# Cross scores as three fp32r products, decay rows fetched by ScalarE into one buffer, value products a unit later

## The chip, the cores and the metric

One core of one Trainium2 chip runs the kernel. The metric is the device time of one execution in microseconds (us), lower is better. TensorE (PE in the profile) multiplies matrices into PSUM, VectorE (DVE) and ScalarE (ACT) work elementwise, GpSimd (POOL) does small statistics, and SyncE (SP) issues most DMAs.

## The reference

Four encoder layers over 256 tokens of width 1024, all in fp32. Each layer is a mixer (a Mamba-2 state space mixer, differential attention, spatial gating, the state space mixer again) beside a cross attention to a memory of 256 rows; both are concatenated, projected and added to x, and a squared-ReLU MLP follows. The two parts that the change touches:

```python
def memory_cross_attention(q, mem_n, w_kv, gq, gk):      # 4 heads of 256
    k, v = jnp.split(mem_n @ w_kv, 2, axis=-1)
    q = rmsnorm(q.reshape(b, l, X_HEADS, X_HEAD_DIM), gq)
    k = rmsnorm(k.reshape(b, m, X_HEADS, X_HEAD_DIM), gk)
    s = jnp.einsum('blhd,bmhd->bhlm', q, k) * (X_HEAD_DIM ** -0.5)
    p = jax.nn.softmax(s, axis=-1)
    return jnp.einsum('bhlm,bmhd->blhd', p, v)

# ssd_chunked: within a chunk, per group g and head r
y_diag = jnp.einsum('bcgls,bcgrls,bcsgrp->bclgrp', cb, segsum_exp(adt), xdt)
```

`segsum_exp` is the exponential of a difference of cumulated sums, for every pair of positions. The kernel builds it from a "decay row" (the cumulated sums of one head along the free axis, on all partitions) less a per-partition column.

## The kernel before, in words

All weights are a stream of 570 units of 128 x 1024 fp32 (512 KB). SyncE loads unit u into `raw` (6 slots). ScalarE rounds it to fp32r in `w_hi_t` (line 1434, ring of 4), VectorE takes the rest, raw less high, into `w_lo_t` (line 1678), and TensorE multiplies each unit as three fp32r products: activations high x weights high, high x weights low, low x weights high (lines 1236 to 1238 for form `nat`, 1247 to 1249 for form `feat` with 256 columns, 1258 and 1265 for `wide`). A `nat` unit is 12 matmuls of 512 columns.

A planner in Python (class `Plan`, from line 112) writes one list of steps. Every engine goes through this list in order and does its own part of each step. Small work (transposes, norms, attention heads, state space groups) are Python generators, "threads", that advance once per weight unit: `yield 2` waits two units. A step placed at unit w is preceded on ScalarE and VectorE by the casts of the units up to w + 2, so each engine prepares weights about three units ahead of TensorE. `is_late` delays a step while the planner's summed costs (`COST`) for an engine lie over a limit. PSUM has 8 banks: pairs (0,1) and (2,3) alternate for weight units (`stream_job`), banks 4 to 7 are `misc` for small work. A `Job` holds banks and knows when ScalarE and VectorE have read them (counted in `act_free`, `dve_free`); the next user of the bank waits for that (`banks_free`).

The parts that matter here:

- **Keys and queries.** `normed` (line 304) multiplies four units into a pair of banks. `row_norm` then runs squares (ScalarE, line 1516), the inverse root (GpSimd), the product (VectorE, lines 1747 and 1749, step `norm_mul`), and two steps `nt_turn`: TensorE transposes (1293) and ScalarE copies to `qT` (1503) or `kT` (1506), both plain fp32. VectorE has no part in `nt_turn`.
- **A cross head** (`head`, line 333): `x_score` is four fp32 matmuls of 128 x 256 (line 1383), two token tiles x two halves of the 256 features; then `x_exp` (ScalarE 1623), `x_norm` (VectorE 1907, 1910), `x_turn` (TensorE 1392, ScalarE 1628, VectorE 1915 makes `xpT_lo`), and one unit later `x_out`: twelve fp32r matmuls of 128 x 256 against the values `v`, `v_lo` (1404 to 1406).
- **The first units.** The list begins with values 0 (units 0 to 3), values 1 (4 to 7), keys 0 (8 to 11), keys 1 (12 to 15). Values 0 and keys 0 share banks (0,1). The values' evacuation is ScalarE line 1529 and VectorE line 1922; it needs the memory's inverse root from GpSimd.
- **State space groups** (`ssm`, 8 groups in each of two layers). After step `decay`, ScalarE stores the cumulated sums to HBM (`cs_rows`, 1555). Step `ssd_r` is SyncE's: it waits for that store, and from the third group on for the exponentials of the group two before (`e_new`), and issues two broadcast loads of 256 KB into `gap[n % 2]` (line 1045), between two weight loads in its own order. `gap` has two pairs of buffers; the second pair lies in tiles 22 and 23 of `act_hi` and `act_lo`. Step `ssd_gap` on VectorE subtracts the column (line 1791, 8 instructions), placed in the same unit as `ssd_a` of the group before it. `ssd_a` has on ScalarE the two exponentials into `E` (1567), on VectorE `cbm` (1796); `ssd_m` multiplies (1802, 1807), `ssd_b` is TensorE's 1334 and 1340.
- **Output projection** (`out_projection`, line 484): two accumulators a and b of two banks; units go tile 0 a, tile 0 b, tile 1 a, tile 1 b, and so on.

## Time and profile before

| | us |
|---|---|
| median of 3 runs (1770.59 to 1770.93) | 1770.88 |
| the profiled execution, its own time | 1770.17 |
| its span, first to last instruction | 1768.4 |
| TensorE busy (9556 matmul records) | 1760.0 |
| VectorE busy | 1182.3 |
| ScalarE busy | 1005.3 |
| GpSimd busy | 220.0 |

The page gives busy time by engine, the chain of waits that ended last, and groups of like instructions. Matmuls overlap in the array: the duration of one record is longer than its share of TensorE's time, so what a matmul costs is read from the distance between neighbours in the timeline. Where records of one line are merged, "x8" is their number and the second column their stretch.

### The profile page before, as it was taken

How to read it: one execution, taken by the hardware profiler on the slowest of the kernel's cores; microseconds unless marked ns; L12 is line 12 of the kernel's file. 1: busy time of each engine (PE TensorE's matmuls, PEld its weight loads, DVE VectorE, ACT ScalarE, POOL GpSimd, SP SyncE). 2: the span in 40 equal slices, each digit the busy share in tenths (PEclk: the TensorE clock that was granted, in tenths of full speed). 3: DMA queues.
4: the chain of work that ended last, by engine and by line, in shares of the span. 5: the costliest groups of instructions: out<-in, count | busy, mean ns of one | idle time of the engine just before them, and what ended most of it. 6: DMA issues, size and time to landing. Idle time of an engine off the chain costs nothing.

```text
span 1768.4 us, 26013 instructions
## 1 busy us (share of the span) xinstructions
PE 1760.0 (100%) x9556; PEld 1518.9 (86%) x9556; DVE 1182.3 (67%) x1628; ACT 1005.3 (57%) x1598; POOL 220.0 (12%) x548
## 2 busy tenths in 40 slices
PE   9999999999999999999999999999999999999999
PEld 8998988888888888888888888888899998888887
DVE  5788876666665666656566566655678887656665
ACT  6667775544455675544465545444566777545443
POOL 2412231000012220000012300000131223100000
PEclk9999999999999999999999999999999999999999
DMA  7555543555555443555565445555557554355554
GB/s 271 171 204 186 179 143 122 181 190 191 191 186 180 156 141 121 177 191 191 191 213 180 160 136 182 191 191 191 190 168 215 177 173 150 122 190 189 191 191 143
DMA packets 90041, 314.03 MB, mean 178 GB/s; under 512 B 10176, under 2 KB 11584, under 8 KB 89920
## 3 DMA queue, kind: packets, MB, share of 16 engines
q1 hardware_dynamic: 89328, 311.27, 53.0%
q8 instruction: 80, 1.31, 0.3%
q10 hardware_dynamic: 592, 1.12, 0.2%
q14 instruction: 41, 0.34, 0.1%
HBM read 311.23 MB, written 1.11 MB: 177 GB/s over the span
## 4 chain that ended last, share of the span: by engine, by line
PE 96%; DVE 3%; ACT 1%; issue 1%; ACTq 0%; DVEq 0%
PE ps L1236 19%; PE ps L1238 19%; PE ps L1237 19%; PE ps L1258 13%; PE ps L1265 7%; PE ps L1247 3%; PE ps L1248 3%; PE ps L1249 3%; PE ps L1283 1%; PE ps L1383 1%; PE ps L1334 1%; PE ps L1293 1%; DVE w_lo_t L1678 1%; DVE xsT L1761 1%; DVE bcT L1761 1%
## 5 line engine op out<-in xcount | busy, mean ns | idle before, releaser
L1678 DVE TENSOR_TENSOR w_lo_t<-raw,w_hi_t 128x1024 fp32r<-128x1024 f32 x569 | 691.7, 1225 | 367.6 <-ACT w_hi_t L1434 367.0
L1434 ACT ACTIVATE w_hi_t<-raw 128x1024 fp32r<-128x1024 f32 x569 | 596.9, 1059 | 393.5 <-PE ps L1238 148.5
L1236 PE MATMUL ps<-w_hi_t,act_hi 128*128 128x512 f32 x832 | 327.7, 394 | 0.6 <-issue 0.6
L1237 PE MATMUL ps<-w_lo_t,act_hi 128*128 128x512 f32 x832 | 324.3, 390 | 0.0
L1238 PE MATMUL ps<-w_hi_t,act_lo 128*128 128x512 f32 x832 | 324.1, 390 | 0.0
L1258 PE MATMUL ps<-hT,w_hi_t 128*128 128x512 f32 x1024 | 256.0, 392 | 0.0
L1258 PEld LDWEIGHTS ps<-hT,w_hi_t 128*128 128x128 f32 x1024 | 185.9, 189 | 34.4
L1238 PEld LDWEIGHTS ps<-w_hi_t,act_lo 128*128 128x128 f32 x832 | 156.2, 188 | 33.1
L1236 PEld LDWEIGHTS ps<-w_hi_t,act_hi 128*128 128x128 f32 x832 | 156.4, 188 | 31.6 <-issue 1.0
L1237 PEld LDWEIGHTS ps<-w_lo_t,act_hi 128*128 128x128 f32 x832 | 156.5, 188 | 30.2
L1236 PE MATMUL ps<-w_hi_t,hT 128*128 128x512 f32 x416 | 165.7, 398 | 0.0
L1238 PE MATMUL ps<-w_hi_t,hT 128*128 128x512 f32 x416 | 162.4, 390 | 0.0
L1237 PE MATMUL ps<-w_lo_t,hT 128*128 128x512 f32 x416 | 162.1, 390 | 0.0
L1247 PE MATMUL ps<-hT,w_hi_t 128*128 128x256 f32 x512 | 149.1, 291 | 0.5 <-DVE w_lo_t L1678 0.5
L1265 PEld LDWEIGHTS ps<-hT,w_lo_t 128*128 128x128 f32 x1024 | 139.7, 190 | 10.0
L1249 PE MATMUL ps<-hT,w_lo_t 128*128 128x256 f32 x512 | 144.9, 283 | 0.0
L1248 PE MATMUL ps<-hT,w_hi_t 128*128 128x256 f32 x512 | 144.8, 283 | 0.0
L1265 PE MATMUL ps<-hT,w_lo_t 128*128 128x256 f32 x1024 | 142.8, 282 | 0.0
L1236 PE MATMUL ps<-w_hi_t,memT_hi 128*128 128x512 f32 x252 | 101.5, 403 | 0.9 <-issue 0.8
L1247 PEld LDWEIGHTS ps<-hT,w_hi_t 128*128 128x128 f32 x512 | 98.1, 192 | 2.1 <-issue 1.6
L1248 PEld LDWEIGHTS ps<-hT,w_hi_t 128*128 128x128 f32 x512 | 98.2, 192 | 0.4
L1238 PE MATMUL ps<-w_hi_t,memT_lo 128*128 128x512 f32 x252 | 98.5, 391 | 0.0
(225 smaller groups left out, 2279.2 us busy)
## 6 DMA issues: line engine op xcount, KB each, us to landing
raw<-in_wstream SPq DMA_DIRECT2D x569, 512.0 KB, 3.3
gap<-cs_rows SPq DMA_DIRECT2D x32, 256.0 KB, 4.8
mix<-in_mem SPq DMA_DIRECT2D x4, 256.0 KB, 5.2
x<-in_x SPq DMA_DIRECT2D x1, 1024.0 KB, 9.1
raw<-in_wstream SPq DMA_DIRECT2D x2, 256.0 KB, 4.1
wsT<-in_sgu_wT ACTq DMA_DIRECT2D x1, 512.0 KB, 3.6
sgain<-in_sgu_gain ACTq DMA_DIRECT2D x1, 512.0 KB, 5.9
out<-x SPq DMA_DIRECT2D x1, 512.0 KB, 2.8
```

Source lines behind the costliest of these rows:

```text
L1236: pe.matmul(o, ah, wh[:, n], start=first and c == 0, stop=False)
L1237: pe.matmul(o, ah, wl[:, n], start=False, stop=False)
L1238: mm = pe.matmul(o, al, wh[:, n], start=False, stop=last and c == UK - 1)
L1247: pe.matmul(o, wh[:, n], ah, start=first and c == 0 and f % 2 == 0, stop=False, skip_group_check=True)
L1248: pe.matmul(o, wh[:, n], al, start=False, stop=False, skip_group_check=True)
L1249: mm = pe.matmul(o, wl[:, n], ah, start=False, stop=last and c == UK - 1, skip_group_check=True)
L1258: pe.matmul(o.rearrange("p (a b) -> p a b", a=2), wh[:, n], hT2[:, :, kt, :], start=first and c == 0, stop=False, skip_group_check=True)
L1265: mm = pe.matmul(o[:, 0:SEQ], wl[:, n], hT2[:, 0, kt, :], start=False, stop=last and c == UK - 1, skip_group_check=True)
L1283: mm = pe.transpose(ps[:, bf, f * SEQ + t * P:f * SEQ + (t + 1) * P], src[:, t, (2 * m + f) * P:(2 * m + f + 1) * P], ident)
L1434: act.activation(w_hi_t[:, u % RING, :], raw[:, u % SLOTS, :], ACT.Copy).then_inc(w_hi, 1)
L1678: dve.tensor_tensor(w_lo_t[:, u % SLOTS, :], raw[:, u % SLOTS, :], w_hi_t[:, u % RING, :].bitcast(F32), ALU.subtract)\
L1761: ins = dve.scalar_tensor_tensor(out=dst[:, f, d:SEQ], in0=ps[:, job.banks[h], (f % 2) * SEQ:(f % 2 + 1) * SEQ - d], scalar=col("conv_w", ...
```

## The change

Three things at once. (1) `qT` and `kT` become fp32r high parts; `nt_turn` gets a VectorE step that writes low parts `qT_lo`, `kT_lo` (into tiles 16 to 23 of `act_hi` and `act_lo`, where the heads' results go later); a score is three fp32r products per token tile and feature half, twelve matmuls, and waits for VectorE as well. (2) The decay rows are fetched by ScalarE into one pair of buffers: the first group's in step `ssd_r`, the later ones at the end of the group before's exponentials in `ssd_a`; VectorE's `ssd_gap` and GpSimd's `ssd_xd` move to three units after `ssd_a`. (3) `x_out` is placed two units after `x_turn` in place of one; the very first key block takes banks (6,7); the output projection begins with tile 0 a, tile 1 a, tile 0 b, tile 1 b. The squares of the spatial gating layer get an fp32 view of `qT`'s memory.

```diff
-... "x_score": (0, 0.7, 1.72)
+... "x_score": (0, 0.7, 1.44)
...
             for m in range(2):
-                tj = self.misc_job(True, False)
+                tj = self.misc_job(True, dst in ("qT", "kT"))
+                if tj.dve:
+                    self.work(0, 0.7, 0)
                 self.step("nt_turn", m=m, nt=job.dve, dst=dst, tile=tile + 2 * m, gain=gain, job=tj)
-            self.ready[dst, tile // 4] = tj.act
+            self.ready[dst, tile // 4] = tj
...
-        job = self.stream_job(True, True)
+        job = Job(self, banks, True, True) if banks else self.stream_job(True, True)
...
-        self.normed("mem", ("w_mem_kv", i), n * COLS, 2, ("m", self.r_m), "kT", n, ("xk", i))
+        self.normed("mem", ("w_mem_kv", i), n * COLS, 2, ("m", self.r_m), "kT", n, ("xk", i), (6, 7) if i == n == 0 else None)
...
         self.step("x_turn", n=n, job=pT)
-        yield 1, "x_out"
+        yield 2, "x_out"
...
-        for n in range(last):
+        for n, nb in ((0, 0), (1, 0), (0, 1), (1, 1)):
+            unit(n, (a, b)[nb], nb, False, None)
+        for n in range(2, last):
...
             while self.decay_act is None:
                 yield 1
+            yield 1
             self.step("ssd_r", g=g, l=l, n=l * SG + g)
...
             yield from rows(0)
-            self.spawn(rows(1))
             yield 2
...
                 if g + 1 < SG:
-                    self.spawn(gaps(g + 1))
-                    self.spawn(weighted(g + 1), 1)
-                if g + 2 < SG:
-                    self.spawn(rows(g + 2), 1)
+                    ready["r", g + 1] = True
+                    self.spawn(gaps(g + 1), 3)
+                    self.spawn(weighted(g + 1), 3)
...
+        qT_lo, kT_lo = act_hi[:, CROSS0:CROSS0 + 8, :], act_lo[:, CROSS0:CROSS0 + 8, :]
+        sq = sb("sq", [P, 8, SEQ], F32, o_qT)
-        gap = [[sb("gap00", ...), sb("gap01", ...)],
-               [sb("gap10", ...), sb("gap11", ...)]]
+        gap = [sb("gap0", [P, HPG * P], F32, o_s2), sb("gap1", [P, HPG * P], F32, o_s2 + 2048)]
...  # SyncE
-                while row_steps and row_steps[0]["w"] <= u - SLOTS + 1:
-                    s = row_steps.pop(0)
-                    n = s["n"]
-                    sp.wait_ge(cs_out, 16 * (s["l"] + 1))
-                    if n > 1:
-                        sp.wait_ge(e_new, TT * (n - 1))
-                    for b in range(TT):
-                        ...
-                        sp.dma_start(gap[n % 2][b][:, :], r.partition_broadcast(P)).then_inc(gap_in[n % 2], 16)
...  # TensorE
                     banks_free(s["job"])
-                    pe.wait_ge(act_free, s["qk"])
+                    for job in s["qk"]:
+                        split(job)
                     for t in range(TT):
+                        o, tok = ps[:, s["job"].banks[0], t * MEM:(t + 1) * MEM], slice(t * P, (t + 1) * P)
                         for c in range(2):
-                            mm = pe.matmul(ps[...], qT[:, 2 * s["h"] + c, t * P:(t + 1) * P],
-                                           kT[:, 2 * s["h"] + c, :], start=c == 0, stop=c == 1, skip_group_check=True)
+                            d = 2 * s["h"] + c
+                            pe.matmul(o, qT[:, d, tok], kT[:, d, :], start=c == 0, stop=False, skip_group_check=True)
+                            pe.matmul(o, qT[:, d, tok], kT_lo[:, d, :], start=False, stop=False, skip_group_check=True)
+                            mm = pe.matmul(o, qT_lo[:, d, tok], kT[:, d, :], start=False, stop=c == 1, skip_group_check=True)
...  # ScalarE
+            def spread(l, g):
+                for b in range(TT):
+                    r0 = b * SH + HPG * g
+                    act.dma_start(gap[b][:, :], cs_rows[l, r0:r0 + HPG, :].rearrange("h c -> (h c)").partition_broadcast(P)).then_inc(gap_in, 16)
...
+                    if s["g"] + 1 < SG:
+                        act.wait_ge(e_new, TT * (n + 1))
+                        spread(s["l"], s["g"] + 1)
+                elif k == "ssd_r":
+                    act.wait_ge(cs_out, 16 * (s["l"] + 1))
+                    spread(s["l"], s["g"])
...  # VectorE
+                elif k == "nt_turn" and s["dst"] in ("qT", "kT"):
+                    job, tile = s["job"], s["tile"]
+                    b = job.banks[0]
+                    dve.wait_ge(act_free, job.act)
+                    if s["dst"] == "kT":
+                        ins = dve.tensor_tensor(kT_lo[:, tile:tile + 2, :]..., ps[:, b, :], kT[:, tile:tile + 2, :]....bitcast(F32), ALU.subtract)
+                    else:
+                        i = s["gain"][1]
+                        for f in range(2):
+                            ins = dve.scalar_tensor_tensor(out=qT_lo[:, tile + f, :], in0=ps[:, b, f * SEQ:(f + 1) * SEQ],
+                                                           scalar=gx16[:, 2 * i + f:2 * i + f + 1], in1=qT[:, tile + f, :].bitcast(F32),
+                                                           op0=ALU.mult, op1=ALU.subtract)
+                    ins.then_inc(dve_free, 1)
...
-                    dve.wait_ge(gap_in[n % 2], 32 * (n // 2 + 1))
+                    dve.wait_ge(gap_in, 32 * (n + 1))
```

## Rows read from the trace of the kernel before

**Rows 1.** The page: busy us (share of the span), number of instructions.

```profile
PE 1760.0 (100%) x9556; PEld 1518.9 (86%) x9556; DVE 1182.3 (67%) x1628; ACT 1005.3 (57%) x1598; POOL 220.0 (12%) x548
```

**Rows 2.** TensorE's groups by shape: busy us, mean ns; idle before.

```profile
L1383 PE MATMUL ps<-kT,qT 128*128 128x256 f32 x128 | 30.2, 379 | 0.0
...
L1405 PE MATMUL ps<-xpT_lo,v 128*128 128x256 f32 x64 | 18.1, 283 | 0.0
```

**Rows 3.** TensorE's timeline at a score: start us, duration us, engine, line.

```profile
247.30 1.89 PE L1383 MATMUL ps<-kT,qT 128*128 128x256 f32 x8
...
249.25 0.40 PE L1237 MATMUL ps<-w_lo_t,act_hi 128*128 128x512 f32 x1
```

**Rows 4.** TensorE's timeline at the value products of layer 0, head 1.

```profile
277.70 0.39 PE L1238 MATMUL ps<-w_hi_t,act_lo 128*128 128x512 f32 x1
279.00 0.36 PE L1404 MATMUL ps<-xpT,v 128*128 128x256 f32 x1 [0.91 <-DVE xpT_lo L1915]
279.19 0.28 PE L1405 MATMUL ps<-xpT_lo,v 128*128 128x256 f32 x1
...
280.51 0.40 PE L1236 MATMUL ps<-w_hi_t,act_hi 128*128 128x512 f32 x1
```

**Rows 5.** VectorE's timeline at the same place.

```profile
277.92 0.68 DVE L1915 TENSOR_TENSOR xpT_lo<-ps,xpT 128x512 fp32r<-128x512 f32 x1
```

**Rows 6.** TensorE's timeline at the value products of layer 3, head 1.

```profile
1509.86 0.39 PE L1238 MATMUL ps<-w_hi_t,memT_lo 128*128 128x512 f32 x1
1510.43 0.36 PE L1404 MATMUL ps<-xpT,v 128*128 128x256 f32 x1 [0.18 <-issue]
```

**Rows 7.** TensorE's timeline at the first unit of keys 0 (unit 8).

```profile
30.32 0.39 PE L1238 MATMUL ps<-w_hi_t,memT_lo 128*128 128x512 f32 x1
31.54 0.47 PE L1236 MATMUL ps<-w_hi_t,memT_hi 128*128 128x512 f32 x1 [0.82 <-issue]
```

**Rows 8.** VectorE's timeline at the same place.

```profile
30.03 1.41 DVE L1922 SCALAR_TENSOR_TENSOR v_lo<-ps,stats,v 128x512 fp32r<-128x512 f32 x2 [3.13 <-ACT v L1529]
```

**Rows 9.** TensorE's timeline at unit 45, layer 0.

```profile
145.69 0.39 PE L1238 MATMUL ps<-w_hi_t,hT 128*128 128x512 f32 x1
146.31 0.36 PE L1247 MATMUL ps<-hT,w_hi_t 128*128 128x256 f32 x1 [0.24 <-DVE w_lo_t L1678]
```

**Rows 10.** VectorE's timeline ahead of unit 45.

```profile
132.42 1.65 DVE L1791 TENSOR_SCALAR gap<-gap,cs 128x128 f32<-128x128 f32 x8
...
144.95 2.35 DVE L1678 TENSOR_TENSOR w_lo_t<-raw,w_hi_t 128x1024 fp32r<-128x1024 f32 x2
```

**Rows 11.** TensorE's timeline at unit 209, the first of layer 1's output projection.

```profile
672.71 0.39 PE L1238 MATMUL ps<-w_hi_t,memT_lo 128*128 128x512 f32 x1
673.73 0.47 PE L1236 MATMUL ps<-w_hi_t,act_hi 128*128 128x512 f32 x1 [0.63 <-issue]
```

**Rows 12.** VectorE's timeline at the same place.

```profile
672.23 1.40 DVE L1747 SCALAR_TENSOR_TENSOR nt<-ps,stats 128x512 f32<-128x512 f32 x2
```

**Rows 13.** VectorE's groups by shape: busy us, mean ns; idle before.

```profile
L1729 DVE SCALAR_TENSOR_TENSOR hT<-ps,percol_sb,hT 128x256 fp32r<-128x256 f32 x64 | 26.5, 477 | 17.8 <-ACT hT L1493 17.6
...
L1928 DVE TENSOR_TENSOR act_lo<-ps,act_hi 128x512 fp32r<-128x512 f32 x16 | 11.0, 688 | 19.8 <-ACT act_hi L1632 19.8
```

**Rows 14.** ScalarE's and TensorE's timelines at layer 1, head 0.

```profile
639.08 1.09 ACT L1506 ACTIVATE kT<-ps 128x512 f32<-128x512 f32 x2 [0.66 <-PE ps L1293]
...
642.07 1.89 PE L1383 MATMUL ps<-kT,qT 128*128 128x256 f32 x8
```

**Rows 15.** The decay rows' and their store's transfers: duration ns min/median/max; landing.

```profile
L1045 SPq DMA_DIRECT2D gap<-cs_rows x32: 326/432/1712, 99.1 to 1464.2; - x32
...
DMA to landing us min/median/max: 3.2/4.8/7.4
...
L1555 ACTq DMA_DIRECT2D cs_rows<-csT x2: 463/481/499, 90.6 to 1322.9; - x2
```

**Rows 16.** Busy time of each engine in the state space mixer of layer 0.

```profile
85.00:300.00 215.00, 213.85 (x1342) 192.31 (x1340) 173.12 (x326) 146.56 (x252) 42.58 (x90) 1.00 0.51 169
```

More of the change, by code:

```diff
@@ L302, in row_norm, with normed @@
             self.threads.insert(0, self.turning)
-    def normed(self, src, weight, col, groups, r, dst, n, gain):
-        job = self.stream_job(True, True)
+    def normed(self, src, weight, col, groups, r, dst, n, gain, banks=None):
+        job = Job(self, banks, True, True) if banks else self.stream_job(True, True)
         self.block("nat", src, weight, col, job, lambda: self.row_norm(job, groups, r, dst, 4 * n, gain))
@@ L336, in head @@
             yield 1
-        qk = max(self.ready["kT", h // 2], self.ready["qT", h // 2])
+        qk = (self.ready["kT", h // 2], self.ready["qT", h // 2])
         yield from self.in_order("x_turn", n - 1)
@@ L722, in one @@
             jobs = [self.misc_job(False, True) for _ in range(2)]
-            self.step("d_score", h=h, qk=max(self.ready["dq", h // 4], self.ready["dk", h // 4]), jobs=jobs)
+            self.step("d_score", h=h, qk=max(self.ready["dq", h // 4].act, self.ready["dk", h // 4].act), jobs=jobs)
             yield 1, "d_exp"
@@ L861, in bass_trunk @@
         memT = (sb("memT_hi", [P, 8, MEM], F32R), sb("memT_lo", [P, 8, MEM], F32R))
-        kT = sb("kT", [P, 8, MEM])
+        kT = sb("kT", [P, 8, MEM], F32R)
         v = sb("v", [P, TT, D], F32R)
@@ L869, in bass_trunk @@
         mix = sb("mix", [P, TT, DIN])
-        qT = sb("qT", [P, 8, SEQ])
+        o_qT = here()
+        qT = sb("qT", [P, 8, SEQ], F32R)
         consts = sb("consts_sb", [P, NCN])
@@ L947, in bass_trunk @@
         mem_in = [sem(f"mem_in{m}") for m in range(4)]
-        gap_in = [sem(f"gap_in{m}") for m in range(2)]
+        gap_in = sem("gap_in")
         zeros_in, w0_in, w_half, w0_lo = sem("zeros_in"), sem("w0_in"), sem("w_half"), sem("w0_lo")
@@ L1033, in _ @@
             weights(5)
-            row_steps = [s for s in steps if s["kind"] == "ssd_r"]
             for u in range(SLOTS, NU):
-                while row_steps and row_steps[0]["w"] <= u - SLOTS + 1:
-                    s = row_steps.pop(0)
-                    n = s["n"]
-                    sp.wait_ge(cs_out, 16 * (s["l"] + 1))
-                    if n > 1:
-                        sp.wait_ge(e_new, TT * (n - 1))
-                    for b in range(TT):
-                        r0 = b * SH + HPG * s["g"]
-                        r = cs_rows[s["l"], r0:r0 + HPG, :].rearrange("h c -> (h c)")
-                        sp.dma_start(gap[n % 2][b][:, :], r.partition_broadcast(P)).then_inc(gap_in[n % 2], 16)
                 kind, value = plan.release[u - SLOTS]
@@ L1379, in _ @@
                     banks_free(s["job"])
-                    pe.wait_ge(act_free, s["qk"])
+                    for job in s["qk"]:
+                        split(job)
                     for t in range(TT):
+                        o, tok = ps[:, s["job"].banks[0], t * MEM:(t + 1) * MEM], slice(t * P, (t + 1) * P)
                         for c in range(2):
-                            mm = pe.matmul(ps[:, s["job"].banks[0], t * MEM:(t + 1) * MEM], qT[:, 2 * s["h"] + c, t * P:(t + 1) * P],
-                                           kT[:, 2 * s["h"] + c, :], start=c == 0, stop=c == 1, skip_group_check=True)
+                            d = 2 * s["h"] + c
+                            pe.matmul(o, qT[:, d, tok], kT[:, d, :], start=c == 0, stop=False, skip_group_check=True)
+                            pe.matmul(o, qT[:, d, tok], kT_lo[:, d, :], start=False, stop=False, skip_group_check=True)
+                            mm = pe.matmul(o, qT_lo[:, d, tok], kT[:, d, :], start=False, stop=c == 1, skip_group_check=True)
                     mm.then_inc(job_done, 1)
@@ L1566, in _ @@
                         act.wait_ge(gap_new, TT * n + b + 1)
-                        act.activation(E[:, b, :], gap[n % 2][b][:, :], ACT.Exp).then_inc(e_new, 1)
+                        act.activation(E[:, b, :], gap[b][:, :], ACT.Exp).then_inc(e_new, 1)
                     act.wait_ge(dve_free, jobs["C"].dve)
@@ L1615, in _ @@
                         c = slice(D + s["nb"] * COLS, D + (s["nb"] + 1) * COLS)
-                        ins = act.activation(qT[:, 4 * s["nb"] + 2 * t:4 * s["nb"] + 2 * t + 2, :].rearrange("p a b -> p (a b)"), mix[:, t, c], ACT.Square)
+                        ins = act.activation(sq[:, 4 * s["nb"] + 2 * t:4 * s["nb"] + 2 * t + 2, :].rearrange("p a b -> p (a b)"), mix[:, t, c], ACT.Square)
                     ins.then_inc(sg_sq, 1)
@@ L1732, in _ @@
                     ins.then_inc(dve_free, 1)
+                elif k == "nt_turn" and s["dst"] in ("qT", "kT"):
[3 more added lines that the diff above has]
+                    if s["dst"] == "kT":
+                        ins = dve.tensor_tensor(kT_lo[:, tile:tile + 2, :].rearrange("p a b -> p (a b)"), ps[:, b, :],
+                                                kT[:, tile:tile + 2, :].rearrange("p a b -> p (a b)").bitcast(F32), ALU.subtract)
+                    else:
[5 more added lines that the diff above has]
+                    ins.then_inc(dve_free, 1)
                 elif k == "norm_red":
@@ L1873, in _ @@
                     dve.wait_ge(sg_sq, s["n"])
-                    sq = qT[:, 4 * nb:4 * nb + 4, :].rearrange("p a b -> p (a b)")
-                    dve.tensor_reduce(ssy[:, 8 * nb:8 * nb + 8], heads(sq, 8), AX.X, ALU.add).then_inc(sg_red, 1)
+                    v2 = sq[:, 4 * nb:4 * nb + 4, :].rearrange("p a b -> p (a b)")
+                    dve.tensor_reduce(ssy[:, 8 * nb:8 * nb + 8], heads(v2, 8), AX.X, ALU.add).then_inc(sg_red, 1)
                 elif k == "sgu_scale":
```

6 lines of the change are left out of this document (2 added, 4 removed).

## The prediction, made before the changed kernel was run

> **What bounds the kernel now.** I read the page's busy times first: TensorE is busy for 1760.0 of 1768.4 us [rows 1]. VectorE at 67% and ScalarE at 57% have room on average. So the change can gain in two ways only: less work on TensorE, or fewer of the holes that are left. I then read TensorE's groups by shape [rows 2] and, for the price of one matmul, its timeline, because the records overlap. Last, I went along the timeline for pairs of neighbours further apart than usual, and looked on VectorE for what ended just then [rows 4 to 12]. A hole is measured from end to end: the end of a record less the end of the one before, less the usual step. The usual step is 0.23 us for 512 columns and 0.12 us for 256 columns of fp32r: in the value products the starts at 279.19 and 280.51 are eleven steps apart [rows 4].
>
> **The scores.** One score of before is 8 records (four fp32 matmuls, two records each) whose stretch is 1.89 us with a last record of 0.38 us: (1.89 - 0.38) / 7 = 0.216 us each, 1.73 us for a head [rows 2, 3]. From 247.30 to 249.25 lie the eight and one weight matmul of 0.23: the same 1.72. There are 128 such records, 16 heads: 27.6 us. After the change a head has twelve fp32r matmuls of 256 columns, the very shape and count of the value products, at 0.12 us: 1.44 us, 23.0 us in all. This lies wholly on the path, since TensorE waits for nothing there. Saved: **4.6 us**. It can't well be more or less: 64 records of L1405 and hundreds of other 256-column ones step at 0.12.
> The Trainium skill (FP8 and Floating Point Precision, section TensorE Precision Notes) says that true fp32 takes four passes through the array. By that rule alone three products would cost three quarters of before, 20.7 us, and the estimate of the saving would be 6.9 us; the trace agrees with two passes to a record (0.216 us for 256 columns), but the 256-column fp32r step of 0.12 is over half of that, so I keep 4.6.
>
> **Value products a unit later.** At layer 0, head 1, the end-to-end step is (279.00 + 0.36) - (277.70 + 0.39) = 1.27 us, 1.15 over the usual; VectorE's `xpT_lo` ended at 278.60 [rows 4, 5]. At layer 3, head 1, it is 0.54, a hole of 0.42 [rows 6]. One unit more (2.7 us) covers both: **1.6 us** saved. What is late next: nothing before the head's tile in the output projection, which comes five units after in layer 0, and three or more elsewhere. The next head's `x_turn` waits in the planner for `x_out` of the one before, but the older thread goes first in the same unit. Bounds: 0 (the small work behind it on VectorE shifts along) and 1.6; I take 1.6, since the wait is for one VectorE result that is 0.7 us of work behind its queue.
>
> **First key block in banks (6,7).** Unit 8 starts late: (31.54 + 0.47) - (30.32 + 0.39) = 1.30, a hole of 1.07 us [rows 7]. VectorE ended `v_lo`, the last reader of banks (0,1), at 31.44 [rows 8]. Banks 6 and 7 were last used by the memory's transposes, long read. Saved: **1.1 us**. Price: the four transposes of x, two and two a unit apart, now share banks 4 and 5; ScalarE and VectorE need about 1 us each for one, against 2.7 us between the pairs. I put it at 0.
>
> **Output projection order.** Unit 209 has a hole of (673.73 + 0.47) - (672.71 + 0.39) - 0.23 = 0.87 us [rows 11]. It is the first unit of accumulator a, waiting for `norm_mul`, which ended at 673.63 [rows 12]. The new order gives b a unit more, and a none. So it stays, and the reorder brings 0. Its tile 1 is ready long before.
>
> **The decay rows.** Unit 45 of layer 0 has a hole of 0.47 us that ends with `w_lo_t` [rows 9]. In the 14 us before it VectorE did a group's eight subtractions, 1.65 us, ahead of the weights' low parts [rows 10]; layer 3 repeats it. Three units later that work lies behind the low part of unit 45, which comes 1.65 us sooner. Saved: **0.9 us** (bounds 0 and 0.9, as another piece of work may be in its place). SyncE loses 32 issues and the waits in front of them: worth 0, since weights are loaded six units ahead. ScalarE gains 32 issues. One costs 0.33 to 0.50 us by the ScalarE store and the SyncE loads, 1.71 at worst [rows 15], so about 0.9 us per group, 14 us in all, in front of its next weight cast. In this stage ScalarE is busy 147 of 215 us [rows 16]; I put it at 0, with the reserve of about three units as its cover. The first group's wait for the store comes five units after the store was issued: 0.
> The new wait is VectorE's for the rows. They are asked for after the exponentials, which end 1 to 3 us after `cbm`, then 0.9 us of issues and 4.8 us to landing; the subtraction is due three units, 8.2 to 8.6 us, after `cbm`. Most groups have 1 to 2 us to spare, groups 5 to 6 and 6 to 7 none. With the slowest landing, 7.4 us [rows 15], VectorE stands 1 to 3 us. Behind it in its queue stand the low parts of the third unit ahead.
>
> **VectorE's new work.** 32 pieces of 0.477 us for q (128x256) and 16 of 0.688 us for k (128x512) [rows 13]: 15.3 + 11.0 = 26.3 us on an engine with 586 us free, but 173 of 215 us busy in the state space stage [rows 16]. Like the rows they are taken from, each waits for ScalarE's high part first, up to 19.8 / 16 = 1.2 us. The tightest score is layer 1, head 0: ScalarE ends `kT` at 640.17, the score starts at 642.07 [rows 14]; two low parts of 0.69 us, behind one weight part in the queue, end at 641.8. It just fits, and three other places have more room.
> For all that is new (both waits, ScalarE's issues, a fuller VectorE) nothing in the trace has a price. Below: 0. Above: a hole as large as unit 45's, 0.47 us, at each of 14 refills: 6.6 us. I take **1.0 us**, two such holes, nearer to 0, since in the whole trace TensorE met only a few holes of any kind and the reserve is usually whole.
>
> **Sum.** 4.6 + 1.6 + 1.1 + 0.9 - 1.0 = 7.2 us less than the profiled execution's 1770.17 (span 1768.4 and 1.8 around it): 1763.0. The median of the runs stands 0.7 above that execution, so the forecast is 1763.7 us. With the four-pass rule of the Trainium skill (FP8 and Floating Point Precision) the estimate would be 2.3 lower, 1761.4.
>
> **Rivals.**
> (a) As forecast, all four gains and about 1 us of new holes: 0.70.
> (b) The scores and the first key block gain, the other holes move to neighbours in place of going, since VectorE carries more: 4.6 + 1.1 - 1.0 = 4.7, so 1766.2. For it: the holes sit where VectorE's queue is full. Against: each is one short miss. Chance 0.13; still faster.
> (c) New holes of about 6 us eat the gain: 8.2 - 6.0 = 2.2, so 1768.7, within 0.2% (3.5 us, about what this kernel's measurement can tell from no change). For it: ScalarE's casts now stand behind DMA issues, and VectorE's low parts behind the landing. Chance 0.12.
> (d) Slower. One buffer makes every fetch begin after the exponentials, and VectorE stands at the subtraction until the rows land. With landings of 7.4 us against the median's 4.8 and 1.2 us to spare, it stands 1.4 us at each of 14 refills; if its reserve is spent, as at unit 45, all reaches TensorE: 19.6 - 8.2 = 11.4 us more, 1782.3. It decides from 0.84 us a refill (11.7 / 14). Against it: the reserve was spent at one unit of each such layer only, and the rows' landing now is met while weight loads run beside them just the same. Chance 0.05.
> That three products don't pay at all would need a step of 0.144 us for fp32r at 256 columns; no row has that.
>
> **Numbers.** Faster by over 0.2% (below 1767.3): (a) and (b), less a rest, 0.82. Same: (c) and that rest, 0.13. Slower: 0.05. The low end is all gains and no new hole, 8.2, and unit 209's hole closed too: 1770.88 - 9.1 = 1761.8, rounded to 1761.5. The high end takes in most of (c): 1768.5.
>
> **What would show it.** The scores: 192 records at 0.12 us steps, where 128 at 0.216 were. Holes gone at unit 8, unit 45 and both value products; the one at unit 209 still there, perhaps longer. VectorE busy 26 us more, ScalarE's busy time the same, its queue with 32 issues. VectorE's wait at the subtraction, by the rows' DMA, at the later groups. I am wrong if the scores' steps are not 0.12, if TensorE waits at a score for `kT_lo` or `qT_lo`, or if new holes in the two state space stages sum to over 3 us.

## The result and the profile after

The changed kernel takes **1799.45 us** (median of 4 runs, 1799.02 to 1800.19) against 1770.91 (4 runs, 1770.59 to 1771.09) before: a ratio of 1.0162, interval 1.0149 to 1.0175. It is 28.5 us slower, and the forecast was 7.2 us faster. The span is 1798.3 us.

The page's first rows, to be set against [rows 1]:

```profile
span 1798.3 us, 26213 instructions
PE 1764.9 (98%) x9620; PEld 1524.6 (85%) x9620; DVE 1203.2 (67%) x1676; ACT 1005.6 (56%) x1598; POOL 231.0 (13%) x548
```

Span less busy time is 33.4 us on TensorE, where it was 8.4. So the time is not work. It is holes, on an engine that before the change hardly had any. Measured as in the prediction (end to end less the usual step, all above 0.35 us) they sum to 33.7 us after and 5.5 us before. The difference of 28.2, less 4.6 for the cheaper scores, gives 23.6 of the 29.9 us of span. The rest is TensorE at its lower clock: behind three of the holes, 57 steps took nearly twice their time, which is 6.2 us more (the last section has the rows).

Where the holes are is read best from the start of a weight unit's first matmul in the two traces:

| unit | what begins | before | after | later by |
|---|---|---|---|---|
| 45 | layer 0, the hole of [rows 9] | 146.31 | 145.08 | -1.2 |
| 61 | layer 0, fourth group | 200.93 | 205.68 | 4.8 |
| 81 | output projection, tile 4 | 280.51 | 292.05 | 11.5 |
| 97 | MLP of layer 0 | 334.22 | 351.45 | 17.2 |
| 209 | layer 1, output projection | 673.73 | 690.56 | 16.8 |
| 225 | MLP of layer 1 | 730.31 | 752.36 | 22.1 |
| 461 | layer 3, as unit 60 | 1429.75 | 1448.95 | 19.2 |
| 494 | layer 3, output projection, first head's tile | 1553.86 | 1583.12 | 29.3 |

Up to unit 45 the changed kernel leads by 1.2 us. It loses in the state space stages of layers 0 and 3, and 5 us in the heads of layer 1. Between units 97 and 209 (the first MLP and the start of layer 1) it keeps pace, and from unit 225 to 461 it wins 2.9 us back.

**What came as forecast.** TensorE's groups, shapes kept apart, for [rows 2], then its timeline at the start of unit 8, of unit 45, and of a score:

```profile
L1380 PE MATMUL ps<-kT,qT 128*128 128x256 f32 x64 | 18.2, 284 | 0.0
L1382 PE MATMUL ps<-kT,act_hi 128*128 128x256 f32 x64 | 18.1, 283 | 0.0
L1381 PE MATMUL ps<-act_lo,qT 128*128 128x256 f32 x64 | 18.1, 283 | 0.0
```

```profile
30.57 0.39 PE L1232 MATMUL ps<-w_hi_t,memT_lo 128*128 128x512 f32 x1
30.80 0.39 PE L1230 MATMUL ps<-w_hi_t,memT_hi 128*128 128x512 f32 x1
...
144.86 0.39 PE L1232 MATMUL ps<-w_hi_t,hT 128*128 128x512 f32 x1
145.08 0.28 PE L1241 MATMUL ps<-hT,w_hi_t 128*128 128x256 f32 x1
...
297.00 0.28 PE L1380 MATMUL ps<-kT,qT 128*128 128x256 f32 x1
...
298.32 0.28 PE L1382 MATMUL ps<-kT,act_hi 128*128 128x256 f32 x1
```

From 297.00 to 298.32 are eleven steps: 0.12 us each, and no idle time stands before a score, so TensorE never waits for a low part there. Unit 8 begins at 30.80 and unit 45 at 145.08, both without a hole, against [rows 7, 9].

**The rows' landing.** From the tile `gap` (its instructions, its idle time, who waited for it, its DMA):

```profile
L1438 ACTq DMA_DIRECT2D gap<-cs_rows x32: 326/394/1612, 102.6 to 1529.3; - x32
...
  ACT E L1570: 2.9, 4
...
DMA to landing us min/median/max: 3.1/4.7/7.1
```

Issue and landing are as [rows 15] had them. VectorE is not listed as waiting for the DMA at all. So rival (d), whose sign is the right one, is wrong as a mechanism.

**The hole in front of unit 61.** TensorE, then VectorE:

```profile
199.97 0.60 PE L1334 MATMUL ps<-xw,cb 128*128 128x256 f32 x2
205.68 0.55 PE L1241 MATMUL ps<-hT,w_hi_t 128*128 128x256 f32 x1 [5.11 <-issue]
```

```profile
202.89 2.69 DVE L1784 SCALAR_TENSOR_TENSOR xsT<-ps,percol_sb,xsT 128x255 f32<-128x255 f32 x6
205.49 1.22 DVE L1687 TENSOR_TENSOR w_lo_t<-raw,w_hi_t 128x1024 fp32r<-128x1024 f32 x1
```

Unit 61 writes banks (0,1). Their last reader is the second half of a convolution, whose six VectorE instructions end at 205.58; 0.1 us later TensorE starts. "issue" only says that the view saw no cause; the end on the other engine shows it. The hole is 5.54 us. That half convolution was planned in unit 58 before and is planned in unit 61 now, in the very unit in which its banks are wanted.

**The hole in front of unit 81**, TensorE and VectorE again:

```profile
288.15 0.63 PE L1277 MATMUL ps<-consts_sb,mix 128*128 128x128 f32 x4 [1.57 <-DVE xpT_lo L1938]
292.05 0.77 PE L1230 MATMUL ps<-w_hi_t,act_hi 128*128 128x512 f32 x1 [3.27 <-issue]
292.62 0.63 PE L1231 MATMUL ps<-w_lo_t,act_hi 128*128 128x512 f32 x1
...
298.67 0.40 PE L1231 MATMUL ps<-w_lo_t,act_hi 128*128 128x512 f32 x1
298.90 0.39 PE L1232 MATMUL ps<-w_hi_t,act_lo 128*128 128x512 f32 x1
```

```profile
287.93 1.65 DVE L1814 TENSOR_SCALAR gap<-gap,cs 128x128 f32<-128x128 f32 x8
289.49 0.42 DVE L1845 TENSOR_TENSOR cbm<-ps,stats 128x256 f32<-128x256 f32 x1
289.94 0.43 DVE L1849 TENSOR_TENSOR xs<-xs,cbm 128x256 f32<-128x256 f32 x1
290.40 0.76 DVE L1853 TENSOR_TENSOR mix<-mix,xs 128x256 f32<-128x256 f32 x2
291.08 0.87 DVE L1738 SCALAR_TENSOR_TENSOR act_lo<-ps,percol_sb,act_hi 128x256 fp32r<-128x256 f32 x2
```

Tile 4 of the projection's input comes from a group's output. Its low part (L1738) ends at 291.95 and unit 81, which multiplies it, starts at 292.05: holes of 1.81 and 3.81 us in a row. And here the moved subtraction stands directly in front, 1.65 us of it. Why everything falls into one unit is seen in the planner's list of steps (not a trace; w is the unit at which a step is placed):

```
                         before                          after
ssd_a, groups 0 to 7     34 40 48 55 63 69 74 79         35 44 50 56 66 73 78 83
ssd_gap, groups 0 to 7   33 34 40 48 55 63 69 74         34 38 47 53 59 69 76 81
conv tile 8, 2nd half    w58                             w61
turn of input tile 4     w78                             w81

steps placed at w81
before: x_out, x_exp
after:  ssd_b, x_turn, ssd_gap, ssd_xd, group_scale, x_exp, ssd_o, turn (tile 4),
        group_scale, x_norm
```

A group cannot begin before its subtraction, and the subtraction now waits three units behind the group before. The groups run up to four units late. The projection's unit 81 has a fixed place in the list, so the planner drives all threads on until tile 4 is there: small work that stood in units 74 to 82 before lies in one. Layer 3 repeats the hole in front of the convolved block (4.89 us, at 1458.52), but not the one in front of tile 4: there eight units of value blocks stand ahead of the projection, tile 4 is first read at unit 490, and its turn is placed at 485.

### The profile page after: what moved, and what is told of

Read it like the earlier page. It is cut to its first block, busy times and chain, and to the rows that moved or that the text cites. A ratio compares the mean times of both kernels' runs of the same rounds, so it can differ in the third digit from the quotient of the medians.

```text
span 1798.3 us, 26213 instructions
## 1 busy us (share of the span) xinstructions
PE 1764.9 (98%) x9620; PEld 1524.6 (85%) x9620; DVE 1203.2 (67%) x1676; ACT 1005.6 (56%) x1598; POOL 231.0 (13%) x548
## 4 chain that ended last, share of the span: by engine, by line
PE 79%; DVE 2%; ACT 1%; issue 1%; POOL 0%; ACTq 0%; DVEq 0%
PE ps L1230 16%; PE ps L1232 16%; PE ps L1231 16%; PE ps L1252 13%; PE ps L1259 7%; PE ps L1241 2%; PE ps L1243 2%; PE ps L1242 2%; PE ps L1277 1%; PE ps L1328 1%; PE ps L1287 1%; DVE w_lo_t L1687 1%; PE ps L1404 0%; PE ps L1403 0%; PE ps L1402 0%
## 5 line engine op out<-in xcount | busy, mean ns | idle before, releaser
L1252 PEld LDWEIGHTS ps<-hT,w_hi_t 128*128 128x128 f32 x1024 | 185.9, 189 | 34.4
L1259 PEld LDWEIGHTS ps<-hT,w_lo_t 128*128 128x128 f32 x1024 | 139.7, 190 | 10.0
L1241 PEld LDWEIGHTS ps<-hT,w_hi_t 128*128 128x128 f32 x512 | 100.5, 196 | 11.8 <-issue 11.4
L1242 PEld LDWEIGHTS ps<-hT,w_hi_t 128*128 128x128 f32 x512 | 100.6, 196 | 0.3
L1243 PEld LDWEIGHTS ps<-hT,w_lo_t 128*128 128x128 f32 x512 | 100.4, 196 | 0.0
```

The source lines that it names most:

```text
L1241: pe.matmul(o, wh[:, n], ah, start=first and c == 0 and f % 2 == 0, stop=False, skip_group_check=True)
L1242: pe.matmul(o, wh[:, n], al, start=False, stop=False, skip_group_check=True)
L1243: mm = pe.matmul(o, wl[:, n], ah, start=False, stop=last and c == UK - 1, skip_group_check=True)
L1252: pe.matmul(o.rearrange("p (a b) -> p a b", a=2), wh[:, n], hT2[:, :, kt, :], start=first and c == 0, stop=False, skip_group_check=True)
L1259: mm = pe.matmul(o[:, 0:SEQ], wl[:, n], hT2[:, 0, kt, :], start=False, stop=last and c == UK - 1, skip_group_check=True)
```

## The experiments

All are timed against the kernel before in the same session (1770.6 to 1771.0). An undone part is the diff reversed; of the larger edits the core is shown.

**1. Scores back to fp32.** The changed kernel with `qT`, `kT`, four fp32 matmuls and the planner's costs as before; parts 2 and 3 stay.

```diff
-                            pe.matmul(o, qT[:, d, tok], kT[:, d, :], start=c == 0, stop=False, skip_group_check=True)
-                            pe.matmul(o, qT[:, d, tok], kT_lo[:, d, :], start=False, stop=False, skip_group_check=True)
-                            mm = pe.matmul(o, qT_lo[:, d, tok], kT[:, d, :], start=False, stop=c == 1, skip_group_check=True)
+                            mm = pe.matmul(o, qT[:, d, tok], kT[:, d, :], start=c == 0, stop=c == 1, skip_group_check=True)
```

> The changed kernel with the scores back as plain fp32 (no low parts on VectorE, planner costs as before); rows by ScalarE into one buffer, three units later, and the new order stay. Theory A (the late placement of the decay rows' subtraction stretches the chain of state space groups): scores cost 4.6 us more, layer 1 gets its 5 us back, the two state space layers keep most of their 28 us; 1790 to 1799 us. Rival B (VectorE's new low parts are what is too much): at or below 1778 us.

Measured: 1788.71 (1787.4 to 1790.69), ratio 1.0101 (1.0086 to 1.0116). With part 1 gone, the planner's entry included, the kernel is 10.7 us *faster* than the changed one, and 17.9 are still lost. That is 1.3 us below the range of theory A and far from rival B's 1778. Most of the loss is not from the scores, but part 1 costs where it should have saved; experiment 7 parts the 10.7 us in two.

**2. Subtraction at once.** The single buffer stays.

```diff
-                    self.spawn(gaps(g + 1), 3)
-                    self.spawn(weighted(g + 1), 3)
+                    self.spawn(gaps(g + 1))
+                    self.spawn(weighted(g + 1), 1)
```

> The changed kernel with the subtraction placed in the unit of the group before's ssd_a again and GpSimd's part one unit later, the buffer still single, so VectorE stands until the rows land. Theory A: the chain is back to near its old pace, the 5.5 and 4.9 us holes ahead of units 61 and 462 go, but VectorE stands some 5 us at each of 14 refills, of which a part reaches TensorE: 1780 to 1795 us. Rival C (ScalarE's issues and the single buffer itself cost the time, not the placement): no better than 1799 us, rather worse.

Measured: 1844.67 (1838.52 to 1849.09), ratio 1.0414 (1.039 to 1.0437). What VectorE waited for:

```profile
DVE gap L1814 <- DMA gap<-cs_rows: 86.0, 14, 6.8
```

Theory A's 1780 to 1795 is missed, and the time is where rival C put it. Here is the wait of rival (d): 14 refills, 86.0 us of waiting, 6.1 us each (I had priced 1.4, but with the three units in front of it). Kernel 11 below has the same list of steps, but for the fetches and the first group of each state space layer, which is a unit sooner, and its buffers are filled ahead: it takes 1778.26, 66 us less. It is this wait that the three units buy off. With one buffer there are two prices, and the change pays the smaller.

**3. Part 3 undone.** `yield 1, "x_out"`, the first key block in (0,1), the old order.

```diff
-        yield 2, "x_out"
+        yield 1, "x_out"
...
-        for n, nb in ((0, 0), (1, 0), (0, 1), (1, 1)):
-            unit(n, (a, b)[nb], nb, False, None)
-        for n in range(2, last):
+        for n in range(last):
```

> The changed kernel with part three undone: value products one unit after the turn, keys 0 in the old banks, tiles a b a b in the output projection. Theory A: the first keys' hole of 1.1 us comes back and little else moves: 1797 to 1803 us. Rival D (value products a unit later bunch the end of the state space layers): below 1793 us.

Measured: 1796.98 (1795.97 to 1799.14), ratio 1.0148 (1.0133 to 1.0164). The expectation had only the first keys' hole coming back. Beside parts 1 and 2, part 3 costs 2.5 us, where it saves 4.7 alone (experiment 9) and 4.6 beside part 2 (experiment 1 against 5). With it undone the hole at unit 81 is 2.27 us in place of 3.81, and one of 1.25 us at unit 210 is missing. So the same edit has either sign, by the list it is put into.

**4. The half convolution never put off.** `yield 1, "conv"` lets the planner delay the second half while its sum for VectorE is over the limit.

```diff
-            yield 1, "conv"
+            yield 1
             job.read_act(self)
```

> The changed kernel in which the second half of a convolution is never put off by the planner's load. Theory A: it goes back from unit 61 to 58 (and from 462 to 459), so the holes of 5.5 and 4.9 us ahead of those blocks go, the rest stays: about 1789 us, 1786 to 1793. Rival B or C: the same work is still there, so the hole moves elsewhere: 1797 us or more.

Measured: 1786.04 (1784.68 to 1787.16), ratio 1.0084 (1.0067 to 1.0101): 13.4 us of the 28.5 are back by one word. The holes above 0.35 us sum to 8.7 us less, and the steps at the lower clock cost 2.4 us in place of 6.2. Unit 61 starts 0.3 us earlier than before the change, not 4.8 later. In its place is a smaller hole in front of the transposes of the convolved tile:

```profile
199.82 1.10 PE L1308 MATMUL ps<-consts_sb,xsT 128*128 128x128 f32 x8 [1.83 <-ACT xsT L1546]
```

**5. Part 2 alone.** The kernel before, with one buffer, ScalarE's fetches and the subtraction three units later.

```diff
-                    self.spawn(gaps(g + 1))
-                    self.spawn(weighted(g + 1), 1)
-                if g + 2 < SG:
-                    self.spawn(rows(g + 2), 1)
+                    ready["r", g + 1] = True
+                    self.spawn(gaps(g + 1), 3)
+                    self.spawn(weighted(g + 1), 3)
```

> The kernel before with part two alone: decay rows by ScalarE into one buffer, subtraction three units later; fp32 scores, old order. Theory A: most of the loss is here, the chain of groups stretched by up to 4 units: 1785 to 1793 us. Rival B (the low parts on VectorE are the cause): within 4 us of the kernel before.

Measured: 1793.34 (1791.88 to 1796.09), ratio 1.0128 (1.0113 to 1.0143). Part 2 alone loses 22.7 us, at the upper edge of what was expected, with the scores and VectorE's work as before. Nor does VectorE wait for the landing here. Its holes at unit 81 are those of the changed kernel to the hundredth:

```profile
287.37 0.63 PE L1273 MATMUL ps<-consts_sb,mix 128*128 128x128 f32 x4 [1.57 <-DVE act_lo L1944]
291.27 0.76 PE L1226 MATMUL ps<-w_hi_t,act_hi 128*128 128x512 f32 x1 [3.27 <-issue]
```

**6. The scores' price on TensorE alone.** The kernel before, with a score as twelve fp32r matmuls that take the high parts of q and k three times each. This replaces the low-part products, so the output is another one; VectorE gets no new work.

```diff
+                            for m in range(3):
+                                mm = pe.matmul(o, qT[:, d, tok], kT[:, d, :], start=c == 0 and m == 0, stop=c == 1 and m == 2, skip_group_check=True)
```

> The kernel before with each score as twelve fp32r matmuls that all take the high parts (no low parts are computed, the output is not the reference's): TensorE's part of the three products alone. All theories: 16 heads x (8 x 0.216 - 12 x 0.12) = 4.6 us less than before, 1766.2 us, 1765.5 to 1767.

Measured: 1766.92 (1766.65 to 1767.23, 10 runs), ratio 0.9978 (0.9969 to 0.9987): 3.7 us less. Its list of steps is that of the kernel before. In its trace a step is 0.12 us, which saves 4.6 in all, and the value products' holes have grown, from [rows 4, 6]'s 1.15 and 0.42 to 1.41 and 0.70:

```profile
277.10 0.39 PE L1239 MATMUL ps<-w_hi_t,act_lo 128*128 128x512 f32 x1
278.66 0.36 PE L1406 MATMUL ps<-xpT,v 128*128 128x256 f32 x1 [1.18 <-DVE xpT_lo L1917]
```

A faster TensorE arrives sooner at the same late operand: 0.54 us of the 4.6 went back there.

**7. The planner's entry alone.** The work on the chip stays; only the planner no longer counts it.

```diff
                 tj = self.misc_job(True, dst in ("qT", "kT"))
-                if tj.dve:
-                    self.work(0, 0.7, 0)
```

> The changed kernel without the 0.7 that the planner adds to VectorE's load for each new low part; the work itself stays. Theory A2 (in layer 1 the planner's number, not the work, moves the heads from unit 207 to 211): layer 1's 5 us come back, the hole ahead of unit 61 shrinks by a unit's distance: 1788 to 1794 us. Rival (the work itself): 1799 us.

Measured: 1793.64 (1792.59 to 1796.66), ratio 1.013 (1.0115 to 1.0145): 5.8 us less than the changed kernel. The loss in layer 1 is gone (units 209 to 225: -0.9 us against before, where the changed kernel has +5.2). Counting the work truthfully pushed the first head's value product there from unit 208 to 211, into the head of the projection. The half convolution of experiment 4 moves too: part 2 alone takes it from unit 58 to 60, where the hole in front of unit 61 is 1.87 us (2.93 in this kernel), and only the entry takes it to 61. Against experiment 1, which has the same parts 2 and 3, this kernel is 4.9 us slower: the low parts take more than the cheaper scores give.

**8. One buffer saved in another way.** The subtraction's operands land in the buffer of the exponentials, of which there are now two (4 KB each, the memory of one pair of rows and one `E`). The exponential works in place, SyncE fetches two groups ahead as before, and the groups keep their old places. Three products, part 3, no planner entry.

```diff
-        gap = [sb("gap0", [P, HPG * P], F32, o_s2), sb("gap1", [P, HPG * P], F32, o_s2 + 2048)]
-        E = sb("E", [P, TT, HPG * P], F32, o_s2 + 4096)
+        E = [sb("E0", [P, TT, HPG * P], F32, o_s2), sb("E1", [P, TT, HPG * P], F32, o_s2 + 4096)]
...
-                        act.activation(E[:, b, :], gap[b][:, :], ACT.Exp).then_inc(e_new, 1)
+                        act.activation(E[n % 2][:, b, :], E[n % 2][:, b, :], ACT.Exp).then_inc(e_new, 1)
...
-                    self.spawn(gaps(g + 1), 3)
-                    self.spawn(weighted(g + 1), 3)
+                    self.spawn(gaps(g + 1))
+                    self.spawn(weighted(g + 1), 1)
```

> Three products, value products a unit later and the new order as in the changed kernel, no planner cost for the low parts, but two buffers again in the same 8 KB: the exponentials are written in place, SyncE fetches the rows of the group after next once TensorE has read the buffer, the subtraction is where it was. The list of steps has the pace of before. Theory A: the loss is gone and the gains forecast are there: 1763 to 1767 us. Rival B: VectorE's 26 us more of work still cost, 1775 us or more.

Measured: 1766.18 (1765.78 to 1766.43, 8 runs), ratio 0.9973 (0.9963 to 0.9984). It beats both kernels. Its list of steps, the fetches aside, is exactly that of experiment 9, so next to that kernel (1766.29) the products with their low parts cost as much as they save. Two new holes of 1.87 us are seen, one in each state space stage:

```profile
188.85 1.95 PE L1337 MATMUL ps<-xdt,E 128*128 128x128 f32 x16
192.33 0.67 PE L1343 MATMUL ps<-xw,cb 128*128 128x256 f32 x2 [1.53 <-issue]
```

```profile
190.22 1.22 DVE L1683 TENSOR_TENSOR w_lo_t<-raw,w_hi_t 128x1024 fp32r<-128x1024 f32 x1
191.36 1.66 DVE L1748 SCALAR_TENSOR_TENSOR act_hi<-ps,stats,qT 128x256 fp32r<-128x256 f32 x4
```

The group's last product goes to bank 5, just used by the first transposes of q. Before, ScalarE's copy freed it; now VectorE's low part must be done too, the first two of the four instructions of L1748, which stand behind a weight part. Two more, of 0.90 and 0.44 us, are in layer 1, where the low parts of q stand in front of what VectorE owes the transposes of differential attention. Whether working in place costs anything by itself was not timed alone.

**9. Part 3 alone**, on the kernel before.

```diff
-        yield 1, "x_out"
+        yield 2, "x_out"
```

> The kernel before with the third part of the change alone: value products two units after the transposes, the first key block in banks (6,7), the output projection's new order. The list of steps of the groups is the same as before. My prediction's terms for it were 1.6 + 1.1 + 0 = 2.7 us less than before. Theory A (the holes sit where I put them and close): 2.2 to 3.0 us below before. Rival B (they move to neighbours, as half of the value-product gain did not show in the kernel with three products of high parts alone, where that hole grew): 1 to 2 us below. Either way nothing of the change's loss of 28.5 us comes from here; if this kernel is slower than before, both are wrong.

Measured: 1766.29 (1765.77 to 1767.18, 9 runs), ratio 0.9974 (0.9964 to 0.9984): 4.7 us less, more than the 2.7 of the forecast and than either case expected. The holes at both value products and unit 8 are gone; so are two of 0.52 us at the last head's transposes, which I had not listed, and unit 209's went from 0.87 to 0.42 (by the reorder or by the later value product; the two were not timed apart):

```profile
670.53 0.39 PE L1240 MATMUL ps<-w_hi_t,memT_lo 128*128 128x512 f32 x1
671.10 0.47 PE L1238 MATMUL ps<-w_hi_t,act_hi 128*128 128x512 f32 x1 [0.19 <-issue]
```

(671.10 + 0.47) - (670.53 + 0.39) - 0.23 = 0.42.

**10. ScalarE issues, nothing moved.** The kernel before, where step `ssd_r` is ScalarE's in place of SyncE's, with both pairs of buffers.

```diff
+                elif k == "ssd_r":
+                    n = s["n"]
+                    act.wait_ge(cs_out, 16 * (s["l"] + 1))
+                    if n > 1:
+                        act.wait_ge(e_new, TT * (n - 1))
+                    for b in range(TT):
...
+                        act.dma_start(gap[n % 2][b][:, :], r.partition_broadcast(P)).then_inc(gap_in[n % 2], 16)
```

> The kernel before with one thing of the second part: ScalarE issues the two fetches of each group's decay rows, at the same place of the list, into the same two pairs of buffers. Placement of the subtraction and of the groups is unchanged. Theory A (the loss comes from the placement three units later, which stretches the chain of groups): within 1.5 us of before, as each issue costs ScalarE 0.33 to 0.5 us. Rival B (ScalarE's queue, with casts behind DMA issues of up to 1.6 us, loses time by itself): 3 to 20 us slower than before, with TensorE waiting for high parts of weights in the two state space stages.

Measured: 1770.85 (1770.6 to 1771.56, 10 runs), ratio 1.0 (0.999 to 1.0009). ScalarE's 32 issues cost nothing within that interval, as forecast. The list is that of the kernel before. So what costs in part 2 is the placement that goes with the single buffer. The later subtraction was not timed with both pairs of buffers; for it speak the two lists of steps, and that no engine waits for the rows' landing in the traces of the changed kernel and of part 2 alone.

**11. The kernel of 8 with the planner's entry.**

```diff
+                if tj.dve:
+                    self.work(0, 0.7, 0)
```

> The kernel with exponentials in place (three products, third part, fetches by SyncE two groups ahead) that ran at 1766.2, with the change's entry of 0.7 for VectorE per transposed block put back into the planner's sums. The work on the chip is the same; only the list of steps moves. Theory A (the planner's entry alone moves the heads of layer 1 and a half convolution and costs time): 4 to 9 us slower than without it, so 1770 to 1775, most of it in layer 1's units 209 to 225 and near units 61 and 462. Rival B (the entry matters only together with the later subtraction): 1765 to 1768.

Measured: 1778.26 (1777.38 to 1778.65), ratio 1.004 (1.0025 to 1.0055): 12.1 us more than without it, for no other work (11.7, if each is taken against the kernel before in its own session). It is more than either case expected. Layer 1 has its 5.2 us again; the rest is a convolution put off, as in 4, which makes a new hole of 2.89 us at unit 69 (and one at 470, behind which the clock falls):

```profile
225.88 0.39 PE L1243 MATMUL ps<-w_hi_t,hT 128*128 128x512 f32 x1
228.93 0.47 PE L1241 MATMUL ps<-w_hi_t,hT 128*128 128x512 f32 x1 [2.65 <-ACT nt L1525]
```

**12. The bank freed sooner.** The kernel of 8, the first block of queries transposed one unit earlier.

```diff
             self.step("norm_mul", job=job, groups=groups, r=r, n=n)
-            yield 2
+            yield 1 if (dst, tile) == ("qT", 0) else 2
```

> The same kernel of 1766.2 with the first block of queries transposed one unit sooner (one unit after its norm, not two). In the trace of that kernel TensorE stands 1.87 us at 192.78 and at 1422.15: the group's last product takes the bank that the query's transposes have just used, and now has to wait for VectorE's new low part as well. Theory A: both holes close and nothing else moves: 3 to 3.8 us less, 1762.4 to 1763.2, the first below my prediction's 1763.7. Rival B (the low part goes in front of other work of VectorE and makes a hole there): 1765 to 1767.

Measured: **1763.98** (1763.63 to 1764.23), ratio 0.996 (0.9945 to 0.9975). The hole shrank from 1.87 to 0.72 us:

```profile
188.62 1.95 PE L1337 MATMUL ps<-xdt,E 128*128 128x128 f32 x16
190.95 0.67 PE L1343 MATMUL ps<-xw,cb 128*128 128x256 f32 x2 [0.39 <-issue]
```

```profile
187.39 2.68 DVE L1780 SCALAR_TENSOR_TENSOR xsT<-ps,percol_sb,xsT 128x255 f32<-128x255 f32 x6
189.99 1.65 DVE L1748 SCALAR_TENSOR_TENSOR act_hi<-ps,stats,qT 128x256 fp32r<-128x256 f32 x4
```

The low parts now stand behind a half convolution of 2.68 us. The time lies between the ranges of the two cases, so neither had it whole. It is the fastest kernel of the study, 35.5 us below the changed one and 7.0 below the kernel before, and it contains the scores and part 3 of the change in full.

## Why the prediction was wrong

**The step that failed is the one on the decay rows**: "Three units later that work lies behind the low part of unit 45 ... Saved: **0.9 us** (bounds 0 and 0.9 ...". Unit 45's hole did close (145.08 is one usual step behind its neighbour). But I took the list of steps as fixed and one piece of work as shifted in it. The subtraction is a link of a chain: the next group can't start without it. In the code before, it is placed *in the same unit* as the group in front, so it never set the pace; with three units it does. Shown alone, part 2 is worth +22.7 us (experiment 5), not -0.9, and no bound of mine held that. I asked what the new wait would do on the engines and never asked when the next group would be placed, though the diff has the numbers, and the last groups have a fixed date: unit 81 reads tile 4.

**The second failure is a part of the diff that I didn't price: `self.work(0, 0.7, 0)` and the planner's costs.** They are no instruction, so I gave them nothing. The planner puts off what it takes to be too much for VectorE, though VectorE is a third idle. The entry costs 5.8 us in the changed kernel (7) and 12.1 in the kernel with the groups in place (11).

**"I take 1.0 us", for the waits, ScalarE's issues and a fuller VectorE, was too small already for the low parts alone.** Their amount was near: the low parts take 23.6 us by their own groups (20.9 more in the page's total), 26.3 forecast. In a list that is otherwise good they cost 4 to 5 us: part 3 alone and the scores' matmuls alone save 4.7 + 3.7 = 8.4, and kernel 8, with both, saves 4.4. Two holes of 1.87 us are most of it, those of 0.90 and 0.44 in layer 1 the rest. The mechanism of the two large ones is one I had not thought of: not the score waits for the low part, but the next user of the bank. My upper bound of 6.6 held it. Beside part 2 they cost about 8.6 (1793.64 against 1788.71, and 3.7 of TensorE's time given back); in the two traces the holes differ by 6.2 us and the steps at the lower clock by 2.3.

**Parts and whole.** Part 1's matmuls -3.7, part 2 +22.7, part 3 -4.7 sum to +14.3; the change has +28.5. The other 14.2 are, but for rounding and the sessions, the planner's entry (5.8) and the low parts beside part 2 (8.6, as above). Parts 2 and 3 do add up: 22.7 - 4.7 = 18.0, and experiment 1, which has both, measured 17.9. It is part 1 that does not add.

**What was right.** The scores: 0.12 us a step, 4.6 us. An fp32 matmul of before, two records of 0.216 us, is worth 3.6 such steps. The estimate by the four-pass rule of the Trainium skill (FP8 and Floating Point Precision, section TensorE Precision Notes), 6.9 us, was too high: the steps in the trace of experiment 6 save 4.6, and its time is 3.7 lower. The holes at unit 8 and the value products went, part 3 brought even 2 us more than its terms: two holes of 0.52 that I had not listed, 0.45 at unit 209, where I had expected nothing, and a rest that I can't place. That surplus is luck, not forecast. ScalarE's issues cost nothing that could be measured (10). VectorE never waited for the landing, thanks to the three units.

**Of the rivals**, (d) had the sign with the wrong mechanism and the wrong size, in two ways: the wait it named is absent in the changed kernel, and where the three units are taken away (2) it is 6.1 us a refill. I had written of (d) that the reserve was spent at one unit only; the changed kernel spends it by placement, not by waiting. The sign of being wrong "if new holes in the two state space stages sum to over 3 us" was the right test: they sum to 26.

What no rival had, and the sum neither, is the clock: 6.2 us of the loss are steps at the lower level behind the holes.

What stays open: why the low parts cost twice as much beside part 2, and what the later subtraction costs with two pairs of buffers. A second pair outside the low parts' tiles was not tried.

## What to carry to other kernels

When a delay is put on a step, look in the code for what may start only after it, and walk that chain to its first fixed date; a step "moved behind other work" costs nothing only if nothing of the sort follows. Where a planner writes the order, its cost numbers are code with a price: build the list before and after and compare it by kind of step, before any duration is read. A new reader of a bank is a new wait for whoever uses the bank next, however early its result is needed elsewhere. And where a buffer is to be saved, try working in place first: here it moved no step but the fetches (kernel 8).

## What the hardware showed

TensorE's clock was granted in full from 6 to 1766 us of the run before. In the changed kernel it fell to half three times, in the holes in front of units 61, 81 and 462. Windows of its trace (TensorE busy, weight loads, VectorE, ScalarE, GpSimd, then the granted clock, DMA share, GB/s); the last is a neighbour at full clock:

```profile
204.50:211.20 6.70, 5.52 (x26) 5.55 (x27) 3.69 (x8) 0.00 (x0) 0.00 (x0) 0.50 0.02 4
289.90:296.50 6.60, 4.45 (x11) 3.51 (x12) 3.80 (x10) 2.40 (x7) 0.00 (x0) 0.50 0.01 2
1457.20:1463.90 6.70, 5.38 (x25) 5.41 (x26) 3.84 (x8) 0.00 (x0) 0.00 (x0) 0.50 0.01 2
301.00:304.00 3.00, 3.00 (x25) 2.91 (x24) 0.43 (x1) 0.81 (x3) 0.00 (x0) 1.00 0.53 172
```

Ahead of the first fall the engine had stood since 200.6, ahead of the third since 1454.1; by the second it had stood for most of the time since 286.6. The steps behind the first hole:

```profile
206.03 0.41 PE L1242 MATMUL ps<-hT,w_hi_t 128*128 128x256 f32 x1
206.24 0.41 PE L1243 MATMUL ps<-hT,w_lo_t 128*128 128x256 f32 x1
```

Here 24 steps of 256 columns take 0.213 us, the lower level of 1.2 GHz, where 0.12 is usual at the upper of 2.4 GHz: 2.2 us more. From 292.62 to about 296.5 nine steps of 512 columns take 0.427 us in place of 0.23, 1.8 us more. The Trainium skill (TensorE: Matmul & The Clock Gate, part 1) gives 426.7 ns between starts at 512 columns when cold, and the trace agrees. Behind the third hole it is again 24 steps of 256 columns and 2.2 us. So the hole of 3.8 us in front of unit 81 cost 5.6, and the three falls together 6.2 us. I had not expected that in a kernel whose TensorE is 98% busy.
